# Delta rule stage of a one-core transformer kernel: the transposed running inverse by a turn and a copy instead of a second product

## The reference, cut to what matters

```python
kk = jnp.einsum('bhncd,bhnmd->bhncm', k, k)
a_mat = jnp.where(strict, beta[..., :, None] * kk * decay, 0.0) + jnp.eye(CHUNK)
rhs = jnp.concatenate([v * beta[..., None], k * (beta * jnp.exp(g_cum))[..., None]], axis=-1)
sol = lax.linalg.triangular_solve(a_mat, rhs, left_side=True, lower=True, unit_diagonal=True)
u, w = sol[..., :dv], sol[..., dv:]
```

## Time and profile before

| | us |
|---|---|
| median of 3 runs | 4077.54 |
| lowest and highest | 4071.85, 4081.19 |
| the profiled execution | 4077.74 |
| its span | 4076.0 |
| the span of the delta stage, first table load to end of its last tile's solve, about | 797 to 1036 |
| TensorE busy in the span | 3456.4 (85%) |
| VectorE, ScalarE, GpSimd busy | 1973.0, 1146.0, 1094.6 |

### The profile page before, as it was taken

One profiled execution on the slowest core, in us unless ns is written; L12 is line 12 of the kernel. 1 busy time (PEld: TensorE's weight loads), 2 busy tenths in 40 slices (PEclk: granted clock), 3 DMA queues, 4 the chain that ended last, 5 costly groups with the idle time before them and its releaser, 6 DMA issues. The chain is left out here.

```text
span 4076.0 us, 48349 instructions
## 1 busy us (share of the span) xinstructions
PE 3456.4 (85%) x18500; PEld 2683.1 (66%) x18516; DVE 1973.0 (48%) x3347; ACT 1146.0 (28%) x2077; POOL 1094.6 (27%) x606
## 2 busy tenths in 40 slices
PE   6697898599767879899999958899797898998978
PEld 4376666499656657688787846667565776665656
DVE  3599577755432343554545464133355231334543
ACT  3344455333211111100000022133354022333540
POOL 2122000044235333553434303211100332211012
PEclk9798999699888989899999978999899999998989
DMA  3011000000211111321213102100001121100011
GB/s 104 27 32 31 28 5 1 7 1 1 73 42 52 31 31 38 123 93 62 93 62 99 55 1 89 42 16 22 13 4 53 42 78 42 27 11 14 3 63 67
DMA packets 228785, 171.02 MB, mean 42 GB/s; under 512 B 42224, under 2 KB 215840, under 8 KB 227840
## 3 DMA queue, kind: packets, MB, share of 16 engines
q1 hardware_dynamic: 226016, 167.81, 13.4%
q10 hardware_dynamic: 2592, 0.81, 0.1%
HBM read 151.66 MB, written 16.93 MB: 41 GB/s over the span
## 5 line engine op out<-in xcount | busy, mean ns | idle before, releaser
L1440 DVE TENSOR_TENSOR I-15110S<-I-15110S,c_causal 128x256 f32<-128x256 f32 x64 | 27.7, 432 | 459.9 <-PE I-15110S L1378 459.9
L770 DVE TENSOR_TENSOR I-12676act_f<-I-12675act_g,I-12682p_u 128x512 f32<-128x512 f32 x44 | 28.3, 684 | 258.1 <-PE I-12682p_u L265 258.1
L870 DVE SCALAR_TENSOR_TENSOR y_T<-y_T 128x1024 f32<-128x1024 f32 x48 | 140.2, 2971 | 5.4 <-DMA y_T<-in_w_ada 5.4
L756 ACT ACTIVATE I-12675act_g<-I-12681p_g 128x1024 f32<-128x1024 f32 x22 | 22.6, 1028 | 421.9 <-PE I-12681p_g L265 421.9
L261 PE MATMUL I-12681p_g<-hf_hi,I-12657w_hi 128*128 128x512 f32 x352 | 109.5, 392 | 5.0 <-POOL hf_lo L479 5.0
L263 PE MATMUL I-12681p_g<-hf_lo,I-12657w_hi 128*128 128x512 f32 x352 | 109.2, 392 | 0.0
L265 PE MATMUL I-12681p_g<-hf_hi,I-12659w_lo 128*128 128x512 f32 x352 | 109.0, 391 | 0.0
L265 PE MATMUL I-12682p_u<-hf_hi,I-12660w_lo 128*128 128x512 f32 x352 | 108.4, 389 | 0.0
L263 PE MATMUL I-12682p_u<-hf_lo,I-12658w_hi 128*128 128x512 f32 x352 | 108.4, 389 | 0.0
L261 PE MATMUL I-12682p_u<-hf_hi,I-12658w_hi 128*128 128x512 f32 x352 | 108.3, 389 | 0.0
L1320 POOL TENSOR_TENSOR I-15100w_hi<-I-15098w_raw,c_ones 128x1024 fp32r<-128x1024 f32 x16 | 30.3, 1892 | 270.2 <-PE I-15114half L1331 189.8
(11 more groups left out here) (1154 smaller groups left out, 10257.4 us busy)
## 6 DMA issues: line engine op xcount, KB each, us to landing
y_T<-in_w_ada SPq DMA_DIRECT2D x48, 512.0 KB, 3.3
saved_x<-x_T SPq DMA_DIRECT2D x3, 4096.0 KB, 13.6
x_T<-saved_x SPq DMA_DIRECT2D x3, 4096.0 KB, 15.7
I-12655w_raw<-in_w_gate SPq DMA_DIRECT2D x22, 512.0 KB, 4.4
I-12656w_raw<-in_w_up SPq DMA_DIRECT2D x22, 512.0 KB, 4.1
I-15098w_raw<-in_w_in SPq DMA_DIRECT2D x16, 512.0 KB, 3.8
I-15099w_raw<-in_w_in SPq DMA_DIRECT2D x14, 512.0 KB, 3.8
I-12669d_raw<-in_w_down SPq DMA_DIRECT2D x11, 512.0 KB, 4.9
```

What stands on the lines that cost most here:

```text
L770: nc.vector.tensor_tensor(act_f[:, cols], act_g[:, cols], p_u[:, h, :], ALU.mult).then_inc(product, 1)
L870: self.nc.vector.scalar_tensor_tensor(out=self.raw[s], in0=self.raw[s], scalar=1.0, in1=self.c_row, op0=ALU.mult, op1=ALU.mult, accum_out= ...
```

## The change

The first level stays, but for the second product: it doubles T only, since N comes from GpSimd. From level 2 on, N of the level before is made from T by a TensorE transpose of each head into the form 1 half of `p_TN[g]`, right behind the products of `below`, and a 128x256 copy by ScalarE into form 1 of `TN`, right behind the copy of Y of the same group. `double` has one product for each head: T Y at levels 1 to 5, and at level 6 the transposed form only, since only N is used after it. `subtract` handles the one form, 128x256. Two pairs of semaphores are added; `double` waits for the copy of N, and so does `subtract`.

```diff
+    TURNS = STEPS - 1
+        t_turned, n_copied = st.two("t_turned"), st.two("n_copied")
 below:
                             last = mm(p_Y[g][:, h, :], c_T[level - 1][:, h, :], t_of(n, h), start=True, stop=True)
                         last.then_inc(y_done[g], 1)
+                        if level > 1:
+                            for h in heads[GROUPS[g]]:
+                                last = turn(p_TN[g][:, 1, h % 2, :], t_of(n, h), ident)
+                            last.then_inc(t_turned[g], 1)
 double:
                         wait(pe, doubled[g], STEPS * n + level - 1)
+                        wait(pe, n_copied[g], TURNS * n + level - 1)
                         for h in heads[GROUPS[g]]:
-                            mm(p_TN[g][:, 0, h % 2, :], n_of(n, h), Y[:, h, :], start=True, stop=True)
-                            last = mm(p_TN[g][:, 1, h % 2, :], Y[:, h, :], n_of(n, h), start=True, stop=True)
+                            if level < STEPS:
+                                last = mm(p_TN[g][:, 0, h % 2, :], n_of(n, h), Y[:, h, :], start=True, stop=True)
+                            else:
+                                last = mm(p_TN[g][:, 1, h % 2, :], Y[:, h, :], n_of(n, h), start=True, stop=True)
 copy_below:
                         copy(halves(Y, g), halves(p_Y[g], g)).then_inc(y_copied[g], 1)
+                        if level > 1:
+                            act.wait_ge(t_turned[g], TURNS * n + level - 1)
+                            copy(TN[n % 2][g][:, 1, :, :], p_TN[g][:, 1, :, :]).then_inc(n_copied[g], 1)
 subtract:
                             dve.wait_ge(doubled[g], STEPS * n + level - 1)
-                        v.tensor_tensor(TN[n % 2][g][:, :, :, :], TN[n % 2][g][:, :, :, :], p_TN[g][:, :, :, :], ALU.subtract).then_inc(doubled[g], 1)
+                            dve.wait_ge(n_copied[g], TURNS * n + level - 1)
+                        form = 0 if level < STEPS else 1
+                        v.tensor_tensor(TN[n % 2][g][:, form, :, :], TN[n % 2][g][:, form, :, :], p_TN[g][:, form, :, :], ALU.subtract).then_inc(doubled[g], 1)
```

## The result

The changed kernel takes 4037.68 us (median of 4 runs, 4036.11 to 4040.71) against 4075.31 us before (4 runs). The ratio is 0.991, with a 95% interval of 0.9897 to 0.9923: 37.6 us faster, where 23.7 were forecast.

The account below looks back on a forecast made before the run. TensorE was taken to bound the kernel, busy 26.14 of a 26.85 us tile. Six middle tiles at 2.9 us less (17.5) plus first and last (6.2) gave 23.7 us off 4077.74: 4054 us, range 4045 to 4066.

Parts of the forecast that it names:

- The sign: The whole kernel gets faster, chance 0.88; same 0.07; slower 0.05.
- the wait at level 5: In middle tiles, TensorE's stall before level 6's `below`, released by VectorE, would be 1.08 us, against 0.86 before.
- The rest: Later stages begin behind a barrier and move as they are; no DMA is moved; no gain counted there.
- TensorE's prices: Per tile: 24 products removed at 0.223 us, 20 transposes added at 0.11, net 3.1 us less, down to 22.7.
- The copies: Ten ScalarE copies added a tile, 3.8 us, hidden at levels 3 to 5; cost taken as 0.1 us.
- rival (a): At level 5 VectorE slips ahead of GpSimd: 6 x 1.0 us more gain, 4048 us; chance 0.22.
- The waits of the kernel before: Middle tile: 1.03 us of TensorE waits, 0.86 after `turn_keys` and 0.17 within the following `below`.
- First and last tile: Edge tiles of the stage gain 0.9 us at level 1, 0.4 to 0.5 at each other level, 3.1 each.
- (b): ScalarE's copies show at five levels, 0.3 us each: 1.5 us a tile lost, 12 in all, 4066; chance 0.11.
- (c): On TensorE a turn costs a product: net 4 x 0.22 us a tile, 7 in all, 4071; 0.07 with unforeseen losses.
- (d): In the delta stage transposes lower TensorE's clock from 2.4 to 1.2 GHz: slower, 4100 to some 4235 us; chance 0.05.

Follow-up runs that it names:

- the pair early: `first_inverse` moved ahead of level 4's subtraction on VectorE: in the changed kernel 4041.15 us (ratio 0.9924), in the kernel before 4064.79 us (ratio 0.9988).
- the late pair: Changed kernel with one idle 128x256 VectorE multiplication between the masks and the last two instructions of `first_inverse`: 4046.42 us, ratio 0.9937.
- the repeats: The changed kernel measured twice more without edit: 4040.59 us (ratio 0.9926) and 4045.50 us (ratio 0.9923) against the kernel before.
- the run with products: Changed kernel with the 20 turns of a tile made as products against the identity instead of transposes: 4061.46 us, ratio 0.9975 to the kernel before.

## Why the prediction was wrong

The sign and the way the gain is made were right. From profiled execution to profiled execution the forecast was 16 us short, 39.8 against 23.7, and two steps failed. One is a term of the sum, the wait at level 5 under *VectorE*: put at 1.08 us a tile, it measured 0.26. The other is in *The rest* and the range: everything outside the stage was to "move as they are", at nothing, and it moved by 8.7 us.

The stage's 31.1 us alone, off the 4077.74 on which the forecast was built, would give 4046.6, inside the range. It took the chance outside the stage to leave it.

- **TensorE's prices**: right. A turn is 0.11, a product 0.223, 24 products less and 20 turns more. The tile without waits was put at 22.7 us and is 22.76 with the pair early.
- **The copies**: 0.1 us a tile was taken, and none shows in the changed kernel: levels 3 to 5 last 4.45, 4.45 and 3.83 us, the last with the wait of 0.26 in it.
- **VectorE at level 5**: wrong. Both ends stood there, a wait of 1.08 and one of 0.1, and I took 1.08 "since that is what the row shows and 0.09 is little". The row showed a pair that started behind GpSimd; the hand-made schedule of the new kernel said it would start 0.09 ahead, and it started 0.10 ahead. The row's value was carried over while its cause, which the same paragraph named, had been moved away. The wait is 0.26, and 6 x 0.82 = 4.9 us of the 7.4 by which the stage beat its forecast are this; 0.6 are the copies, nearly all the others the first and the last tile. The Trainium skill (SBUF — State Buffer, Who interferes with whom) has the rule: for a VectorE instruction with two inputs in SBUF and a GpSimd one that reads SBUF, "Issue order, not op shape, decides who blocks." The rows above and the late pair agree, 0.42 when 0.10 ahead, 1.50 when 0.23 behind. I did not weigh it, and it would have given rival (a).
- **The waits of the kernel before**: the 0.17 inside level 6's `below` were counted as a wait and left out of the new tile without a word on why. They stay when the queue is out of the way, as group 1's own chain through the 128x512 subtraction, and the shorter subtraction removes them. The sum did not suffer.
- **First and last tile**: 3.1 us each taken "for the same". The last gave 3.6. The first gave 4.3 against the first trace of the kernel before and 2.7 against the second, since the clock rises at another moment in each. A product there costs 0.42 us until it does, and the forecast priced all at 0.22.
- **Outside the stage**: 6.9 us behind it and 1.8 ahead, chance in one trace of each kernel; the repeats give 30.0 and 29.7 us in all. The profiled execution on which the forecast was built also lies 2.4 us over the measured median of 4075.31. The range was to take in rival (a), at 4048, with a spread of 4 to 6 us below it, and ends at 4045, only 3 below. The times of single executions of the kernel before, 4065.0 to 4086.8 in the last set, show that it should have allowed more.
- **Rivals**: (a) happened, worth 0.82 us a tile where it was put at 1.0. (b) did not; there is cover at levels 3 to 5 and little at level 6. (c) is out by the run with products. Its price of 7 us for that case was too small: the run was 13.2 us faster than the kernel before, as its middle tiles lose the waits as well, 1.82 us each. (d) is out by the clock of 1.00 in every middle tile. The stretch of the last stage that spoke against (d) is only one of several; the next one, in the kernel before:

```profile
4065.00:4070.00 5.00, 2.49 (x16) 2.19 (x14) 2.51 (x2) 0.00 (x0) 0.00 (x0) 0.62 0.45 180
```

The clock fell there, to a mean of 0.62, after TensorE had stood for 1.78, 0.21 and 1.67 us between groups of transposes. So the last stage shows transposes at the full clock, and not that they hold it there; the middle tiles show that these turns among products do.

## What to carry to other kernels

Where one unit is full, count its instructions, and then ask which waits of the present schedule depend on the order of two starts: a faster neighbour moves them, and a cost read off the old trace holds only as long as its cause does. Work out who starts first in the new schedule and believe it, even at 0.1 us. In a program of 4 ms compare a change of 30 us by the stage it touches, which repeated to 0.2 us here but for the moment of the clock's rise in its first tile, and not by one execution of the whole, where the kernel before spread over 20.

## What was not expected of the hardware

- Two VectorE multiplications or subtractions with both inputs in SBUF against one of GpSimd: the one of VectorE that starts ahead of GpSimd's runs on, and the next waits until about GpSimd's end. Behind GpSimd's start VectorE's 0.42 us became 1.50, and 0.94 for the next. GpSimd's cut, which starts 0.25 to 0.32 us ahead of the end of one of VectorE's, takes 1.38 to 1.45 us there and 1.26 to 1.28 later in the tile. The wait is not bound to `first_inverse`: with the pair moved early, a mask of it met GpSimd's decay of the queries, which had started 0.06 ahead (VectorE, then GpSimd):

```profile
875.22 0.42 DVE L2822 TENSOR_TENSOR I-6956TN<-I-6972a_mat,I-6992low 128x256 f32<-128x256 f32 x1
875.56 1.50 DVE L2822 TENSOR_TENSOR I-6957TN<-I-6972a_mat,I-6992low 128x256 f32<-128x256 f32 x1
...
875.50 1.28 POOL L2533 TENSOR_TENSOR I-6959q_dec<-x_T,I-6970e_cum 128x512 f32<-128x512 f32 x1 [7.48 <-PE I-6995F L2640]
```

- ScalarE's 128x256 copies out of PSUM, each 0.38 us long, follow each other at 0.26 to 0.28 us when their inputs are ready.
- The same program's first tile differed by 1.6 us (25.60 and 24.00) through the moment at which the clock rose.
